# A two-block transformer kernel on one core: reordered first units, SSD rounds and tail, loops written out, and 56 weight tiles of 516 columns

## What is computed

```python
def short_conv_mixer(h, w_in, conv_w, w_out):            # first block, layer 0
    b_gate, c_gate, u = jnp.split(h @ w_in, 3, axis=-1)
    v = c_gate * u
    conv = sum(conv_w[k] * vp[:, k:k + S] for k in range(CONV_WIDTH))   # vp: v, padded
    return (b_gate * conv) @ w_out

def ssd_chunked(x, dt, a, bmat, cmat):                   # second block, chunks of 128
    cs = jnp.cumsum(dtc * a.reshape(SSD_GROUPS, SSD_HPG), axis=2)
    xdt = xc * dtc[..., None]
    lmat = jnp.exp(jnp.where(causal, cs_t[..., :, None] - cs_t[..., None, :], -jnp.inf))
    y_diag = ...   # (C B^T) * lmat, times xdt
    states = jnp.einsum('bclgn,bclgr,bclgrp->bcgrpn', bc, decay_states, xdt)
    # prev: state before each chunk, by a scan: h = chunk_decay * h + states
    y_off = jnp.einsum('bclgn,bcgrpn,bclgr->bclgrp', cc, prev, jnp.exp(cs))
    return (y_diag + y_off).reshape(bsz, lp, SSD_HEADS, SSD_HEADDIM)

def mixer_block(h, ...):
    u = rmsnorm(h, norm_w)
    z, xbc, dt_raw, q, k, v, g_ssd, g_att = split_cols(u @ w_in, IN_WIDTHS)
    xbc = jax.nn.silu(causal_dwconv(xbc, conv_w, conv_b))               # 4 taps
    y = ssd_chunked(xh, dt, a, bm, cm) + d_skip[:, None] * xh
    y = gated_group_rmsnorm(y, z, ssd_norm_w)            # y * silu(z), RMS over each of 4 groups
    y_ssd = y @ w_ssd_branch
    att = swa_sink_attention(q, k, v, rel_bias, sinks)
    return (sigmoid(g_ssd + gb[0]) * y_ssd + sigmoid(g_att + gb[1]) * (att @ w_attn_branch)) @ w_out
```

## Time and profile before

| | |
|---|---|
| median of 3 runs | 2466.25 us (2465.83, 2466.25, 2468.79) |
| the profiled execution | 2465.58 us, of which the span of the trace is 2463.9 |
| TensorE busy | 2406.0 us, 98% of the span |
| VectorE, ScalarE, GpSimd busy | 1536.5 us (62%), 861.1 (35%), 105.5 (4%) |
| granted TensorE clock | 0.993 of full speed over the span |
| transfers | 240.29 MB |

### The profile page before, as it was taken

One profiled execution on the slowest core, in us unless ns is written; L12 is line 12 of the kernel. 1 busy time (PEld: TensorE's weight loads), 2 busy tenths in 40 slices (PEclk: granted clock), 3 DMA queues, 4 the chain that ended last, 5 costly groups with the idle time before them and its releaser, 6 DMA issues.

```text
span 2463.9 us, 37145 instructions
## 1 busy us (share of the span) xinstructions
PE 2406.0 (98%) x14867; PEld 2122.8 (86%) x14867; DVE 1536.5 (62%) x2811; ACT 861.1 (35%) x1342; POOL 105.5 (4%) x118
## 2 busy tenths in 40 slices
PE   8999999999999999999999999999999999999998
PEld 5888888887889988888888888988998899998997
DVE  6555345356569855445468886887666655883784
ACT  3123222134345533212244771674332333221212
POOL 0000000000012000000001200220100000000000
PEclk9999999999989999999999999999999999999999
DMA  4336223324343103232223522542321222223223
GB/s 152 103 94 150 86 103 127 131 85 131 124 133 73 40 35 103 86 103 85 102 85 105 119 72 87 121 104 73 101 66 66 83 72 99 87 85 136 87 98 107
DMA packets 67962, 240.29 MB, mean 98 GB/s; under 512 B 22398, under 2 KB 33342, under 8 KB 43838
## 3 DMA queue, kind: packets, MB, share of 16 engines
q1 hardware_dynamic: 30784, 199.83, 23.5%
q0 software_dynamic: 6112, 18.83, 4.1%
q10 hardware_dynamic: 30928, 19.69, 3.4%
HBM read 228.41 MB, written 10.09 MB: 97 GB/s over the span
## 4 chain that ended last, share of the span: by engine, by line
PE 90%; DVE 6%; issue 2%; ACT 1%; DMA 1%; DVEq 0%; POOL 0%; ACTq 0%; POOLq 0%
PE ps L1041 43%; PE ps L1337 25%; PE ps L1593 5%; PE ps L1438 3%; PE ps L1291 3%; PE ps L1194 2%; PE ps L1272 1%; DVE wlo L1641 1%; PE ps L1523 1%; PE ps L1497 1%; PE ps L1143 1%; PE ps L1397 1%; PE ps L1399 0%; DVE Y L2181 0%; PE ps L1061 0%
## 5 line engine op out<-in xcount | busy, mean ns | idle before, releaser
L566 ACT ACTIVATE whi<-raw 128x2048 fp32r<-128x2048 f32 (+2 forms) x187 | 349.7, 1870 | 905.0 <-PE ps L1041 468.0
L1641 DVE TENSOR_TENSOR wlo<-raw,whi 128x2048 fp32r<-128x2048 f32 (+3 forms) x208 | 421.7, 2028 | 73.1 <-ACT whi L566 72.5
L1041 PE MATMUL ps<-parts,whi 128*128 128x512 f32 x1360 | 429.1, 397 | 0.9 <-DVE wlo L1641 0.9
L1337 PE MATMUL ps<-parts,whi 128*128 128x264 f32 (+1 forms) x2400 | 406.5, 291 | 4.1 <-issue 1.7
L1337 PEld LDWEIGHTS ps<-parts,whi 128*128 128x128 f32 x2400 | 332.4, 189 | 14.8 <-issue 10.9
L1041 PEld LDWEIGHTS ps<-parts,whi 128*128 128x128 f32 x1360 | 255.0, 188 | 63.1 <-issue 1.6
L1041 PE MATMUL ps<-parts,wlo 128*128 128x512 f32 x680 | 268.8, 395 | 0.0
L1337 PE MATMUL ps<-parts,wlo 128*128 128x264 f32 (+1 forms) x1200 | 243.1, 284 | 0.0
L1041 PE MATMUL ps<-Mhi,whi 128*128 128x512 f32 x512 | 203.0, 396 | 0.0
L1041 PE MATMUL ps<-Mlo,whi 128*128 128x512 f32 x512 | 203.0, 396 | 0.0
L1041 PE MATMUL ps<-Mhi,wlo 128*128 128x512 f32 x512 | 203.0, 396 | 0.0
(11 more groups left out here) (396 smaller groups left out, 3938.3 us busy)
## 6 DMA issues: line engine op xcount, KB each, us to landing
raw<-in_stream SPq DMA_DIRECT2D x187, 1024.0 KB, 4.9
csb<-sums_d POOLq DMA_DIRECT2D x16, 512.0 KB, 5.9
bands<-scratch ACTq DMA_DIRECT2D x7, 1024.0 KB
near<-bands ACTq DMA_DIRECT2D x16, 256.0 KB, 2.7
csf<-sums_d POOLq DMA_DIRECT2D x32, 128.0 KB, 5.8
tabs<-bands ACTq DMA_DIRECT2D x8, 418.0 KB, 4.2
X<-in_x SPq DMA_DIRECT2D x4, 512.0 KB, 10.3
Q_odd<-parts POOLq DMA_DIRECT2D x8, 256.0 KB, 5.0
```

Source lines behind the costliest of these rows:

```text
L566: nc.scalar.activation(whi[:, s, 0:cols], raw[:, s, 0:cols], ACT.Copy).then_inc(hi_done, 1)
L1041: mm = nc.tensor.matmul(out, w[:, s, at], x(k), start=k + j == 0, stop=k == k_tiles - 1 and j == 2)
L1337: mm = nc.tensor.matmul(ps[:, 2 * par + h, 0:w], wt[:, s, at], x[:, k, a + h * w:a + (h + 1) * w], start=k + j == 0, stop=k == k_tiles - 1 ...
L1641: low = nc.vector.tensor_tensor(wlo[:, s, a:b], raw[:, s, a:b], whi[:, s, a:b].bitcast(F32), ALU.subtract)
```

## The change

- **Front.** Unit 0 is loaded in two halves (`FRONT`, 1024 columns each), the second after X's first cut; unit 1 is queued when X's first cut has landed; `rel`, `rel2` and `buckets` go through SyncE's queue behind unit 1 and the meta tokens. The first columns of `vecs` come by ScalarE's queue, the rest and `consts` by GpSimd's. TensorE runs 12 matmuls on a zeroed buffer (`Glo`), then unit 0 with the k steps outermost and both tiles inside; the table products stand in units 2 and 3, in two parts (hi, lo), after GpSimd has rounded `buckets` into `bucketr` and split `rel` into `relp`; ScalarE copies the table.
- **Loops.** ScalarE's and VectorE's loops over the mixer's units, and the loops over the two halves on TensorE, VectorE, ScalarE and GpSimd, are Python loops now.
- **Entry.** The two spreads move into tile 0 of the first half, behind two k steps; VectorE reads tile 0 inside its dt chain; turning dt's tokens moves behind tile 2's low k steps.
- **Rounds.** VectorE adds the state before it reads the other two products.
- **Gating and branch.** At r = 18 the split of the next unit moves ahead of `gated(5)`; tile 19 is read after the second `low_part`; `group_root(1)` follows its variance directly. ScalarE splits that unit after its square root's table load and before it waits for the variance.
- **Widths.** z, branch and pair tiles have 516 columns, from `CUT` = 12 on, where they had 528.
- **Tail.** The roots, diagonals and scalings of the two halves of the final norm stand in another order, the first half's spread after two k steps of tile 7.

The core of the diff (the same `range(2)` loops on the other engines and the slices of 516 columns are left out):

```diff
-            sp.dma_start(raw[:, 0, :], io["stream"][0]).then_inc(landed[0], 16)
+            sp.dma_start(raw[:, 0, 0:FRONT], io["stream"][0][:, 0:FRONT]).then_inc(front_loaded, 16)
             for n in range(X_CUTS):
                 k = slice(n * KT // X_CUTS, (n + 1) * KT // X_CUTS)
                 sp.dma_start(X[:, k, N_META:TOK], io["x"][:, k, :]).then_inc(x_loaded[n], 16)
-            sp.wait_ge(x_loaded[X_CUTS - 1], 16)
+                if n == 0:
+                    sp.dma_start(raw[:, 0, FRONT:], io["stream"][0][:, FRONT:]).then_inc(landed[0], 16)
+            sp.wait_ge(x_loaded[0], 16)
             sp.dma_start(raw[:, 1, :], io["stream"][1]).then_inc(landed[1], 16)
             sp.dma_start(X[:, :, 0:N_META], io["meta"]).then_inc(meta_loaded, 16)
+            sp.dma_start(rel[:, :], io["rel"]).then_inc(tab_inputs, 16)
+            sp.dma_start(rel2[:, :], io["rel2"]).then_inc(tab_inputs, 16)
+            sp.dma_start(buckets[:, :], io["buckets"]).then_inc(tab_inputs, 16)
             with sp.Fori(1, NU // 2) as i:
                 for s in range(2):
 
...
+            pool.wait_ge(x_loaded[1], 16)
+            pool.dma_start(vecs[:, KT:], io["vecs"][:, KT:]).then_inc(vecs_loaded, 16)
+            pool.dma_start(consts[:, :, :], io["consts"]).then_inc(consts_loaded, 16)
+            pool.wait_ge(consts_loaded, 16)
+            pool.wait_ge(tab_inputs, 48)
+            nc.gpsimd.tensor_tensor(bucketr[:, :], buckets[:, :], ones[0:REL2, 0:1].to_broadcast([REL2, TAB]), ALU.mult).then_inc(tab_inputs, 1)
+            for n, (r, rows) in enumerate(((rel, REL), (rel2, REL2))):
+                nc.gpsimd.tensor_tensor(relp[0:rows, n, 0, :], r[:, :], ones[0:rows, 0:HEADS], ALU.mult).then_inc(tab_inputs, 1)
+                pool.wait_ge(tab_inputs, 48 + 2 * n + 2)
...
-            split_high(0, 0)
-            act.wait_ge(vecs_loaded, 16)
+            act.wait_ge(front_loaded, 32)
+            nc.scalar.activation(whi[:, 0, 0:FRONT], raw[:, 0, 0:FRONT], ACT.Copy).then_inc(front_hi, 1)
             for k in range(KT):
                 act.wait_ge(x_loaded[k * X_CUTS // KT], 16)
                 nc.scalar.activation(Hhi[:, k, N_META:], X[:, k, N_META:], ACT.Identity, scale=vec("norm_mix0", k)).then_inc(h_hi, 1)
-            act.dma_start(consts[:, :, :], io["consts"]).then_inc(consts_loaded, 16)
+                if k == 1:
+                    act.wait_ge(landed[0], 16)
+                    nc.scalar.activation(whi[:, 0, FRONT:], raw[:, 0, FRONT:], ACT.Copy).then_inc(hi_done, 1)
             for k in range(KT):
                 if k >= 3:
                     act.wait_ge(sq_add, k - 2)
                 nc.scalar.activation(sq[:, k % 2, N_META:] if k else acc[:, N_META:], X[:, k, N_META:], ACT.Square).then_inc(sq_done, 1)
-                if k == 3:
+                if k == 1:
                     split_high(1, 0)
+            next_unit("conv_in", 0)
+            act.wait_ge(vecs_loaded, 16)
             norm_root(0)
             norm_spread(0)
-            act.wait_ge(tab_copied, len(TAB_CUTS))
-            act.dma_start(scratch, table[:, :]).then_inc(tab_stored, 16)
+
+            def copy_table(n):
+                a, b = TAB_CUTS[n]
...
+            for c in range(1, 12):
+                next_unit("conv_in", c)
+                if c in (1, 2):
+                    for n in range(3 * c - 3, 3 * c):
+                        copy_table(n)
+                if c == 2:
+                    act.wait_ge(tab_copied, len(TAB_CUTS))
+                    act.dma_start(scratch, table[:, :]).then_inc(tab_stored, 16)
...
+            def first_unit():
+                for k in range(KT):
+                    pe.wait_ge(h_hi, k + 1)
+                    pe.wait_ge(front_hi if k < KT // 2 else hi_done, 1)
+                    for j, (w, x) in enumerate(((whi, Hhi), (wlo, Hhi), (whi, Hlo))):
+                        if j == 1:
+                            pe.wait_ge(front_lo if k < KT // 2 else lo_done, 1)
+                        if j == 2:
+                            pe.wait_ge(h_ready, k + 1)
+                        for m in range(2):
+                            at = slice((k * 2 + m) * P, (k * 2 + m + 1) * P)
+                            mm = nc.tensor.matmul(ps[:, m, :], w[:, 0, at], x[:, k, N_META:], start=k + j == 0, stop=k == KT - 1 and j == 2)
+                            if k == KT - 1 and j == 2:
+                                mm.then_inc(mt_full, 1)
+
...
+            def table_product(n):
+                pe.wait_ge(tab_inputs, 48 + 5)
+                if n >= 3:
+                    pe.wait_ge(tab_copied, n - 2)
+                a, b = TAB_CUTS[n]
+                second = b > TAB1
+                rows = REL2 if second else REL
...
+            pe.wait_ge(dve_own, 1)
+            for n in range(12):
+                nc.tensor.matmul(ps[:, 4, :], Glo[:, 0, 0:P], Glo[:, 0, :], start=True, stop=True)
+            first_unit()
+            unit("conv_in", 1, H1, beside={(0, 5): first_sum, (1, 4): lambda: norm_spread(0)})
             for c in range(2, 12):
-                unit("conv_in", c, H1)
+                tables = {}
+                if c in (2, 3):
+                    tables = {(1, 2 * n): (lambda n=n: table_product(3 * (c - 2) + n)) for n in range(3)}
+                unit("conv_in", c, H1, beside=tables)
...
-            spread_tokens(ENTRY, sq[:, 1, :], False)
-            norm_spread(ENTRY_NORM, True)
-
-            with pe.Fori(0, 2) as i:
+
+            def entry_spreads():
+                pe.wait_ge(diag_ready, ENTRY_NORM + 1)
+                spread_tokens(ENTRY, sq[:, 1, :], False)
+                norm_spread(ENTRY_NORM, True)
+
+            for i in range(2):
...
+                    elif r == TOK_AT:
+                        row_tile(r, low)
+                        tokens_turned()
+                        row_tile(r, high)
+                    elif i + r == 0:
+                        row_tile(r, range(0, 2))
+                        entry_spreads()
+                        row_tile(r, range(2, KT))
...
-            out_tile(7, range(8), 1)
+            out_tile(7, range(2), 1)
             last_spread(0)
-            out_tile(7, range(8, n), 1)
+            out_tile(7, range(2, n), 1)
...
+            dve.wait_ge(front_hi, 1)
+            nc.vector.tensor_tensor(wlo[:, 0, 0:FRONT], raw[:, 0, 0:FRONT], whi[:, 0, 0:FRONT].bitcast(F32), ALU.subtract).then_inc(front_lo, 1)
             for k in range(KT):
+                if k == 2:
+                    dve.wait_ge(hi_done, 1)
+                    nc.vector.tensor_tensor(wlo[:, 0, FRONT:], raw[:, 0, FRONT:], whi[:, 0, FRONT:].bitcast(F32), ALU.subtract).then_inc(lo_done, 1)
...
+            dve.wait_ge(mt_full, T0["half"] + 1)
+            nc.vector.tensor_tensor(halves(stg[:, 0, SSD_TAPS - 1:]), product(0), halves(R[:, :]), ALU.mult).then_inc(mt_free, 1)
...
+                    if c < NC - 1:
+                        dve.wait_ge(st_full, i * 8 + (4 * gg + c + 1))
+                        if c == 0:
+                            nc.vector.tensor_copy(Hs[:, :], ps[:, 4, :]).then_inc(h_new, 1)
+                        else:
+                            dve.wait_ge(hd_ready, i * 6 + (3 * gg + c))
+                            nc.vector.tensor_tensor(Hs[:, :], Hd[:, :], ps[:, 4, :], ALU.add).then_inc(h_new, 1)
...
-                    if c == NC - 1:
-                        return
-                    dve.wait_ge(st_full, i * 8 + (4 * gg + c + 1))
...
+                    nc.vector.tensor_tensor(Y[:, q, CUT:], Y[:, q, CUT:], late(stg[:, q % 2, :]), ALU.mult).then_inc(z_new, 1)
...
-                    if r:
+                    if r not in (0, 20) and i + r != 1:
...
+                    if r == 18:
+                        split_low("half", 8, i * 14)
...
                     for q in range(*((0, 7) if r == 19 else (7, 8) if r == 20 else (0, 0))):
                         low_part(q)
+                        if q == 1:
+                            evacuate(19)
                     if r == 20:
                         add_square(7)
                         group_variance(1)
-                    if r and r % 2 == 0:
+                        group_root(1)
+                    if r and r % 2 == 0 and r != 18:
...
             last_variance(0)
+            last_diagonals(0)
             last_tile(6, 1)
-            last_diagonals(0)
             last_add(6, 1)
+            last_scale(0, range(6))
             last_tile(7, 1)
-            last_scale(0, range(1))
+            last_scale(0, range(6, 7))
             last_add(7, 1)
-            last_scale(0, range(1, 6))
+            last_scale(0, range(7, KT))
             last_variance(1)
-            last_scale(0, range(6, 7))
             last_diagonals(1)
-            last_scale(0, range(7, KT))
```

## The result

The changed kernel takes 2450.11 us (median of 4 executions: 2447.18, 2447.35, 2452.86, 2453.20), the kernel before 2466.04 beside it: a ratio of 0.9932, with a 95% interval of 0.9918 to 0.9946. So it is 0.7% faster, by 15.9 us; 2446.5 was predicted, within 2438 to 2455. The profiled execution is one of 2447.35, with a span of 2445.6.

A forecast was written before the change was run, and what follows sets the result against it. TensorE was taken as the bound, other engines counting only where it waits; 5.0 + 2.0 + 4.1 + 4.9 + 2.5 + 1.1 = 19.6 us off 2465.58 gave 2446.0, forecast 2446.5 as median, range 2438 to 2455.

The forecast's parts named there:

- Front: Start of the kernel, units 0 to 2: 5.0 us gained, range 3 to 8.2.
- The first step: Front: unit 0 ends near 18.5 us and unit 1's splits near 19.2, so unit 1 can start then.
- The lock: Front: GpSimd's 4.1 us buckets' copy holds up VectorE's split or adds; in full, the gain is 4.1 us.
- Entry: Entry of the first SSD half: 1.2 us of TensorE's earlier arrival at round 3 survives.
- Rounds: SSD rounds, per half: state's add first gains 1.1 us beside conv tiles and loses 0.7 beside z tiles.
- Narrow tiles: z, branch and pair tiles, 528 to 516 columns: 56 tiles save 4.1 us, bounds 2.5 and 5.
- Branch stage: Branch stage, both halves: earlier root gives 3.7 us, less clock fall 1.2; 4.9 in all, bounds 2 and 7.
- Loop turn: TensorE's turn between halves: both stops go with the loop, 2.5 us; 1.0 if the first is a true wait.
- Tail: Final norm: the second variance's sums are ready 1.1 us earlier and all that follows moves with it.
- A: Front: the buckets' copy finds a gap, so the front gives 8.2 us, total 2443; chance 0.17.
- B: VectorE's chains keep TensorE's gains: rounds 0, branch 2, front 3, sum 12.5 us, total 2453.5; chance 0.17.
- C: Unrolled halves: straight code is read too late, 28 x 0.84 = 23.5 us lost, total 2470; chance 0.04.

The follow-up runs named there:

- the later copy: Changed kernel with GpSimd's copy of the buckets waiting until VectorE's last square sum is done: 2445.63 us, ratio 0.9913.
- the last version: Changed kernel plus later buckets' copy, earlier norm root, later sum, state's add last beside z tiles, branch low parts and ScalarE's YNhi earlier: 2433.40 us, ratio 0.9860.
- experiment 7: Changed kernel with the entry's two spreads back ahead of tile 0, VectorE's order kept: 2451.23 us, ratio 0.9923.
- Experiment 4: Changed kernel with the state's add last in all rounds (first kernel): 2451.71 us; last only beside z tiles (second): 2445.02 us.
- experiment 1: The changed kernel run again without edits: 2448.40 us, ratio 0.9926; the profiled execution took 2452.40.
- experiment 5: Changed kernel with the second group's root behind the next unit's split: 2446.00 us; separately, with tile 19 read behind its round's low parts: 2448.64 us.
- experiment 6: Kernel before the change with only TensorE's loop over the two halves written out: 2465.42 us against 2468.60, ratio 0.9986.
- experiment 2: Changed kernel with the buckets' copy made by ScalarE: 2444.21 us; or left on GpSimd after VectorE's last square sum: 2445.63 us.

## Where the prediction was right and where not

**Front: 5.0 forecast, 0.5 measured.** The first step held: unit 1 starts at 19.49 (19.2). The lock held as well; it cost TensorE 4.39 us. The step that failed is the price of what follows from a wait: I set the copy's cost at no more than its length and kept the clock for a rival with other waits as its cause. Behind the wait the clock fell for 6.8 us, 5.55 of them busy, which is 2.8 us. The 14.1 us from unit 1's start to unit 2's were short too: without the lock they are 16.1 with the later copy and 17.0 with ScalarE's, as a wait of 0.9 for the sums and a clock fall of 3.4 us stand in them, and 14.3 only in the last version, which has neither (unit 2 at 33.04 against the 33.3 worked out). And the table products cost 0.63 us a pair, 3.8 in all, not 2.8: I took the step of a 128-row matmul for these of 33 rows. Why they are dearer, no run shows.

**Entry: 1.2 forecast, 3.5 measured.** The step that failed is a row that I had and didn't read: in the earlier trace rows four products of the spread take 3.78 us, 0.95 each, while the earlier trace rows has two of the same in 1.21. The clock was at 0.50 there before (1297.2 to 1304.0), so `R` and the dt chain behind it came 1.9 us late. Where it doesn't fall, as in the changed kernel and in experiment 7, those 1.9 are gained, and experiment 7 shows that the moved spreads aren't the reason. The other 1.6 is within the forecast for VectorE's read of tile 0 inside the chain (1.1 to 2.2), and it survived in full; no run tested that read by itself. The forecast let the moved spreads cover their wait of 1.44, which they did (0.43 is left), but nothing of that reaches tile 2.

**Rounds: 0.8 forecast for both halves, 2.0 measured.** The direction of both parts was right. The conv rounds gave 2.0 per half instead of 1.1, the z rounds cost 1.0 instead of 0.7. Experiment 4 puts 1.8 of the former on the add's place, so VectorE must have had more slack between rounds than the one gap of 1.08 us that I counted.

**Narrow tiles: 4.1 forecast, 3.6 measured.** The branch tiles went from 5.84 to 5.77, as the earlier trace rows gave. The pair tiles gained only 0.056 each; why less isn't shown.

**Branch stage: 4.9 forecast, 4.4 measured, for partly other reasons.** TensorE's waits per half fell from 4.35 us (`stg`, `YNlo`, `Gr`) to 2.15 (`YNlo` alone). Half 0 gained 3.5, half 1 only 0.9: in half 0 the clock's stretch shrank from 6.8 to 3.4 us, in half 1 one of 3.4 us appeared. How the gain falls on the halves is a matter of the execution: in the trace of experiment 1 it is 1.9 and 2.4, with the clock down for 6.8 us in half 0 and not at all in half 1, and the sum is 4.3. That `Gr` wouldn't be waited for was right; that the wait for the last low part would grow from 1.06 to 2.07, with the clock falling behind it in most traces, was not seen. The 1.85 per half for the earlier root can't be told apart from it: experiment 5 takes the root back and loses only 0.5, the slow matmuls covering the rest. The read of tile 19 was worth nothing, as forecast.

**Loop turn: 2.5 forecast, 2.7 measured**, shown apart by experiment 6. **Tail: 1.1 and 1.5.**

**Rivals.** A (the copy finds a gap, 2443) is what experiment 2 makes by hand: 2444 to 2446. B fell, since the rounds gave more, not less (its terms, by the way, add up to 12.7, not 12.5). C fell: the straight code of the halves has no issue wait. The only one left, 0.8 us, stands at the dt tile ahead of them, as it did before. D was right in kind and place, a clock fall in unit 1, but for another reason and smaller: it came behind the lock's wait, at 26.4, not behind waits for X and unit 1's weights, and took 2.8 us, not 5.

## What to carry to other kernels

Before moving work to an idle engine, look at what its instruction would run beside: a 4 us GpSimd copy made a 0.69 us VectorE sum take 4.18, and starting it 0.7 us later, behind the sum, made that free. A wait of TensorE can cost more than its length: check the granted clock behind each, and read a matmul that takes longer than its twin elsewhere as a stretch at the lower clock before costing anything that follows. When a removed wait brings little, find which wait ends last now: here, in the last version, filling 2 us of idle VectorE time ahead of the last low part, with ScalarE's order to match, gave 4 us per half.

## What the runs showed of the hardware

- The clock's falls are partly a matter of the execution: near 879 TensorE ran 10.24 us at 0.50 in one execution of the changed kernel and none in another, at the same busy share, and that moves the whole by 4.4 us. The last version's four executions lie within 1.2 us, those of the changed kernel within 6; that its fewer waits are the reason isn't shown.
- After waits of 4.4, 2.1 and 0.9 us the clock fell for 6.8, 3.4 and 3.4 us; after one of 1.87 us in experiment 7 it didn't. The same wait doesn't always do the same: of the two of 2.07 us in experiment 1's trace one was followed by 6.8 us at 0.50 and the other by none, and the wait of 0.93 us for the square sums in the first kernel of experiment 4 by none. What decides it, these runs leave open.
- GpSimd's copy, released by the buckets' transfer, started between 23.01 and 24.37 us in eight traces whose kernels have the same code up to there but for the warming matmuls. In five of them it began before VectorE's last sum and that took 4.18 to 4.19 us, in three it began later and the sum took 0.69. Both traces of the changed kernel itself are among the five.
- A stop at a hardware loop's turn can be put down to another engine: 1.48 of the 2.3 us went away with TensorE's loop alone.
